# Start addresses of the feed-forward's two moving operands, 208 and 176 bytes past the weights modulo 256

## The reference

```python
mod = silu(c) @ w_ada + b_ada                       # six shift, scale and gate vectors
h = rms_norm(x, norm_mix) * (1 + sc_a) + sh_a
p = h @ w_in                                        # 2048 x 3912, three groups of heads
o = [mla_attention, stick_breaking_attention, forgetting_attention], each head normed
x = x + g_a * (o @ w_out)
h = rms_norm(x, norm_ffn) * (1 + sc_m) + sh_m
x = x + g_m * (square(relu(h @ w_ff1)) @ w_ff2)     # 2048 x 8192, 8192 x 2048
return rms_norm(x, final_norm)
```

## Time and profile before

| | |
|---|---|
| timed runs | 1144.57, 1148.88, 1174.74 us, median 1148.88 us |
| profiled execution, its own time | 1145.03 us |
| its span, first to last instruction | 1143.2 us |
| mean granted TensorE clock | 0.989 of 2.4 GHz |
| PE busy | 1100.5 us, 96% |
| DVE busy | 724.6 us, 63% |
| ACT busy | 534.5 us, 47% |
| POOL busy | 308.1 us, 27% |
| read from HBM | 293.37 MB, 258 GB/s over the span |

### The profile page before, as it was taken

One profiled execution on the slowest core, in us unless ns is written; L12 is line 12 of the kernel. 1 busy time (PEld: TensorE's weight loads), 2 busy tenths in 40 slices (PEclk: granted clock), 3 DMA queues, 4 the chain that ended last, 5 costly groups with the idle time before them and its releaser, 6 DMA issues.

```text
span 1143.2 us, 21676 instructions
## 1 busy us (share of the span) xinstructions
PE 1100.5 (96%) x9072; PEld 1067.7 (93%) x9072; DVE 724.6 (63%) x931; ACT 534.5 (47%) x672; POOL 308.1 (27%) x149
## 2 busy tenths in 40 slices
PE   7989999998999989999999999999999999999996
PEld 6879999886799978999999999999999999999995
DVE  4588767887875569877786545444555555445453
ACT  4644444666655445444444333333444454344441
POOL 3998897853029970000000000000000000000001
PEclk8999999999999999999999999999999999999998
DMA  9999999988659986888886666565666656665651
GB/s 360 408 399 408 380 367 364 360 336 277 218 201 353 366 330 236 305 301 302 276 277 203 193 195 197 191 197 193 196 189 200 191 187 200 197 191 191 198 183 74
DMA packets 81888, 296.88 MB, mean 260 GB/s; under 512 B 9088, under 2 KB 9216, under 8 KB 81792
## 3 DMA queue, kind: packets, MB, share of 16 engines
q1 hardware_dynamic: 81792, 295.50, 73.6%
HBM read 293.37 MB, written 2.10 MB: 258 GB/s over the span
## 4 chain that ended last, share of the span: by engine, by line
PE 78%; DMA 6%; DVE 5%; POOL 3%; issue 3%; ACT 3%; DVEq 0%; SPq 0%; ACTq 0%
PE ps L1398 47%; PE ps L1404 24%; DMA ada<-in_ada 4%; POOL w_lo L836 3%; PE ps L1416 2%; PE ps L1581 2%; DMA raw<-in_weights 1%; DVE ada L947 1%; PE ps L1421 1%; ACT w_hi L485 1%; POOL ssq L830 0%; DVE qk L1029 0%; ACT o_tok L743 0%; PE ps L1591 0%; PE ps L1440 0%
## 5 line engine op out<-in xcount | busy, mean ns | idle before, releaser
L485 ACT ACTIVATE w_hi<-raw 128x1024 fp32r<-128x1024 f32 x346 | 363.2, 1059 | 435.3 <-PE ps L1404 352.9
L928 DVE TENSOR_TENSOR w_lo<-raw,w_hi 128x1024 fp32r<-128x1024 f32 x254 | 308.7, 1224 | 267.2 <-ACT w_hi L485 266.5
L1398 PE MATMUL ps<-hT,w_hi 128*128 128x256 f32 x3072 | 385.1, 278 | 9.2 <-ACT w_hi L485 3.9
L1398 PEld LDWEIGHTS ps<-hT,w_hi 128*128 128x128 f32 x3072 | 367.5, 189 | 12.6 <-issue 5.5
L1398 PE MATMUL ps<-act,w_hi 128*128 128x256 f32 x2048 | 252.9, 276 | 0.0
L1398 PEld LDWEIGHTS ps<-act,w_hi 128*128 128x128 f32 x2048 | 241.6, 188 | 0.0
L836 POOL TENSOR_TENSOR w_lo<-raw,w_hi 128x1024 fp32r<-128x1024 f32 x92 | 219.9, 2408 | 63.7 <-ACT w_hi L485 63.5
L1404 PE MATMUL ps<-hT,w_lo 128*128 128x256 f32 x1536 | 207.9, 278 | 2.6 <-POOL w_lo L836 1.9
L1404 PEld LDWEIGHTS ps<-hT,w_lo 128*128 128x128 f32 x1536 | 190.4, 189 | 3.3 <-POOL w_lo L836 2.4
L830 POOL TENSOR_TENSOR ssq<-ssq,sq 128x1024 f32<-128x1024 f32 x6 | 14.4, 2403 | 657.3 <-ACT sq L492 657.3
L1404 PE MATMUL ps<-act,w_lo 128*128 128x256 f32 x1024 | 136.9, 276 | 0.0
(11 more groups left out here) (231 smaller groups left out, 822.6 us busy)
## 6 DMA issues: line engine op xcount, KB each, us to landing
raw<-in_weights SPq DMA_DIRECT2D x346, 512.0 KB, 4.3
ada<-in_ada SPq DMA_DIRECT2D x180, 512.0 KB, 6.4
more<-in_weights SPq DMA_DIRECT2D x16, 512.0 KB, 8.4
more<-in_ada SPq DMA_DIRECT2D x12, 512.0 KB, 8.6
xT<-in_xt SPq DMA_DIRECT2D x4, 512.0 KB, 7.4
y<-tmp SPq DMA_DIRECT2D x4, 256.0 KB, 2.5
consts<-in_consts SPq DMA_DIRECT2D x1, 580.0 KB, 11.8
y<-sq SPq DMA_DIRECT2D x2, 256.0 KB, 3.0
```

What stands on the lines that cost most here:

```text
L485: sc.activation(w_hi[:, slot, :, :], raw_room(u0 + j), ACT.Copy).then_inc(hi_done, 1)
L928: ve.tensor_tensor(w_lo[:, slot, :, :], raw_room(u), w_hi[:, slot, :, :].bitcast(F32), ALU.subtract).then_inc(lo_vec, 1)
L1398: pe.matmul(acc[:, n, :], w, rhs[:, kt0 + k, half, :], start=first and k == 0 and n % 2 == 0 and half == 0, stop=False, skip_group_check=True)
```

## The change

`hT` and `act` are no longer tensors of their own but views into tensors 64 elements (256 bytes) longer. The view of hT begins 4 elements (16 bytes) into its room, at byte 120656, and the view of act 60 elements (240 bytes) into its room, at byte 153904. Modulo 256 that is 80 and 48, so their distance past the weights becomes 208 and 176 in place of 192. Tensors behind hT move by 256 bytes and those behind act by 512, so they keep their place modulo 256. In turned units on hT the moving operand starts 48 bytes past the weights in place of 64; products on `lat` and `oT` keep 192 and 64. The order of the instructions is the same on all five engines, with the same semaphores, shapes and loads.

```diff
-        hT = sb("hT", [P, KT, 2, S], F32R)
+        hT_room = sb("hT", [P, KT * 2 * S + 64], F32R)
+        hT = hT_room[:, 4:4 + KT * 2 * S].rearrange("p (k h t) -> p k h t", k=KT, h=2)
...
-        act = sb("act", [P, HALF, 2, S], F32R)
+        act_room = sb("act", [P, HALF * 2 * S + 64], F32R)
+        act = act_room[:, 60:60 + HALF * 2 * S].rearrange("p (k h t) -> p k h t", k=HALF, h=2)
```

## The result

The changed kernel takes 1181.74 us (median of four runs, 1178.46 to 1181.77) where the kernel before takes 1146.72 us: the ratio is 1.0304, with a 95% interval of 1.0278 to 1.0331. It is slower by 3%. Four of the 36 executions of the kernel before that stand beside these runs took 1170 to 1175 us (one of the four here, 1174.74 us) and the others 1140.82 to 1151.52 us; no ratio of this document uses the four, none of them was profiled, and what made them long isn't shown. The forecast was 1148 us within 1122 to 1176, so both the direction and the range were missed. The profiled execution took 1178.46 us, with a span of 1176.7 us, 33.5 us more than the 1143.2 us before.

What follows compares the result with a forecast made beforehand. The prediction took TensorE's matmul pace in the feed-forward as the bound, 6,024 matmuls times a pace. All terms were 0: 1143.2 + 0, or 1145 us for the profiled execution, a forecast median of 1148 us, range 1122 to 1176.

Steps and rivals of the forecast that it cites:

- Terms 1 and 2: Feed-forward matmuls on hT (192 to 208) and on act (192 to 176), 3,072 each: 0 taken for both.
- the quick pace: TensorE in the feed-forward's steady stretch at distance 192: 113.3 ns a matmul, 2.72 us a unit.
- the slow pace: Same matmul form in the mixer's first projection at distance 192: 117.9 ns; +14 us for each feed-forward operand.
- the turned unit's excess: 13.8 ns in units with hT as weights; as upper bound 123.4 ns a matmul, at most +30 us per operand.
- rival D: Pace depends only on how the stream was entered, not on start distance: 1145 to 1149 us; chance within the forecast's 0.34.
- Term 3: Mixer: straight units on hT from 192 to 208, turned units from 64 to 48; 0 taken, 6 us gain to +4 us.
- Term 4: ACT and DVE writing act and w_hi: no dependence of their times on the start, 0.
- Rival A: Feed-forward after its last wait: both operands settle in the slow pace, 27.6 us more, 1173 us; chance 0.27.
- Rival B: Feed-forward: excess of 3.7 ns goes for both operands, with up to 6 us of mixer, 1117 to 1123 us; chance 0.17.
- Rival C: One operand stays, the other moves: +14 us (1159), chance 0.10, or -11 us (1134), chance 0.06.

Runs made afterwards that it cites:

- e1: Changed kernel with act back at distance 192 and hT still at 208: 1164.11 us, ratio 1.0157 to the kernel before.
- e3: Changed kernel with hT, act and the weights w_hi and w_lo all starting 16 bytes on, hT and act at distance 192: 1144.62 us, ratio 0.999 to before.
- e8: Changed kernel with only the offsets differing, hT at distance 16 and act at 144: 1173.15 us in one execution.
- e14: Changed kernel with hT and act both at distance 144: 1178.36 us, ratio 1.0254 to the kernel before.
- e13: Changed kernel with hT and act both at distance 112: 1145.8 us, ratio 0.9996 to the kernel before.
- e11: Changed kernel, distances kept, with the feed-forward's weight load reading one column 128 times: 1151.39 us.
- e12: Changed kernel, distances kept, with the feed-forward's moving operand being one column read 256 times: 1138.69 us.
- e10: Changed kernel with only the offsets differing, hT at distance 80 and act at 196, 4 bytes past 192: 1184.18 us in one execution.

## Why the prediction was wrong

**What bounds the kernel.** Right. The time is 6,024 matmuls times a pace, and the whole result was a change of pace. The feed-forward alone gave 31.6 of 33.5 us.

**Terms 1 and 2.** This is the step that failed: "I take 0 for both: the nearest row is the quick pace itself". The reasoning under it was that the distance runs through all values twice in each matmul, so that a start value only moves a moment. e1 and e3 show that it does more: 208 in place of 192 costs 5.8 ns a matmul on hT in the stretch that is otherwise the same, and moving all three operands together costs nothing. The measured terms are 8.3 + 5.1 = 13.4 us for hT and 18.2 us for act, where I had 0 with an upper value of +14 us by the slow pace and +30 us by the turned unit's excess. The bounds held; the value inside them was chosen by the nearest row, and that row was a special one. Nothing in the trace of before showed how special: every matmul of this form in it had the distance 192, on lat and oT as well. One distance seen is no evidence on the next.

**The two paces.** I saw that one distance had two, and counted rival D, by which only the entry matters, with the forecast (0.34 together). The observation was right, and e8 and e14 confirm it. D wasn't: with the order of the work unchanged, the distance moves the paces. That "a pace, once taken, is kept until a wait or another kind of unit" is too simple as well: without a wait hT went from 119.2 ns in the change's first half to 116.7 in its second, with act between, and in e13 each of the mixer's four long stretches on hT took 11 to 16 steps of up to 130 ns before it settled at 113.3.

**Term 3.** Near: 1.8 us in all ahead of the feed-forward, where I had 0 with -6 to +4. The turned units, from 64 to 48, went to 232.7 ns from 229.6 on average, 192 x 3.1 ns = 0.6 us.

**Term 4.** Right: 1061 and 1226 ns against 1062 and 1226.

**Rival A** had the mechanism's place, its sign and the way it shows (records longer, clock unchanged, no wait), with a chance of 0.27. Its price was 27.6 us because I took the slow pace of distance 192, 117.9 ns, for both operands; at the new distances the paces are 119.2 and 119.3 ns and for a quarter of the matmuls 116.7, 31.6 us. This is also why the range was too short above: its upper end was rival A's 1173 and a little, and the other three timed runs lie at 1181.7 us. They are 3.3 us over the profiled one; hT's second half at 119.2 in place of 116.7 ns would be 1,536 x 2.5 ns = 3.8 us, which fits but wasn't profiled.

**Rival B** has nothing behind it now: at sixteen multiples of 16 the pace is never under 113.3 ns, and with the moving operand's walk taken away altogether it is 111.7, not 109.6. **Rival C** is what e1 made on purpose: 1164 us, where I had 1159.

**The Trainium skill.** "TensorE: Matmul & The Clock Gate", "Step-by-step: what each phase is for", has the weight load take nothing from the running matmul. e11 and e12 disagree for this form: of 119.2 ns 5.9 are gone without the weight load's walk and 7.5 without the moving operand's. The measurement decides. The 16-byte line of "SBUF — State Buffer", "Specifications (TRN2)", fits e10 in sign, where a start 4 bytes off a line gave the slowest pace of the feed-forward, 120.3 ns. But that is only 0.3 ns above the 120.0 of 0 and 96, which start on a line, and no other start off a line was tried: that lines are the cause isn't shown.

## What to carry to other kernels

When a long run of matmuls with a weight load each bounds a kernel, take the start-to-start pace from the timeline and compute the distance between the two operands' starts modulo 256, since 16 bytes made up to 6 ns of difference on 113 here, on every matmul. Search the distances on the chip with one operand each for two phases of one kernel, as here; the map has no smoothness to interpolate on. Then confirm the chosen distance in several executions and in every stretch: 144 looked quick in half of e8 and was slow in all of e14's feed-forward. A tensor added or resized ahead of either operand changes the distance as well, so check it after every change of the allocation.

## What the runs showed of the hardware

The pace of this form (float32r, 128 weight columns, 256 moving columns, full clock) takes separate values between 113.3 and 120.3 ns in the feed-forward, and up to 123.3 ns in the mixer of e3. The start distance modulo 256 decides whether 113.3 ns is within reach: it is at 112 and 192, and sometimes at 144, and it never was at the thirteen other multiples of 16. One distance can have several paces (144: 113.3, 116.7, 118.7; 208: 116.7, 119.2 and, in e3, 117.8, 123.3), and in the feed-forward each, once settled, was held through a stretch of 174 us or more without drift. With the moving operand's walk removed it is 111.7 ns, and with the weight load's walk removed 113.3 ns. What in the memory makes two walks collide, and what picks among the paces of one distance, stays open.
